# A three-block mixer kernel on one core: norm sums by row or by tile, bank and queue order at four norm starts, and the order of work in the mixers' loop

## The reference

```
def rms_norm(x, w):
    xf = x.astype(jnp.float32)
    y = xf * lax.rsqrt(jnp.mean(xf * xf, axis=-1, keepdims=True) + EPS)
    return (y * w.astype(jnp.float32)).astype(x.dtype)
```

```
    inner = jnp.einsum('bnqhd,bnkhd->bnhqk', q, k) * decay
    inner = jnp.einsum('bnhqk,bnkhe->bnqhe', inner, v)
    cross = jnp.einsum('bnqhd,hq,bnhde->bnqhe', q, xi, prev)
    o = (inner + cross).reshape(B, S, H, dh)
    mu = jnp.mean(o, axis=-1, keepdims=True)
    var = jnp.mean((o - mu) ** 2, axis=-1, keepdims=True)
    o = ((o - mu) * lax.rsqrt(var + EPS)).reshape(B, S, H * dh)
```

```
    y_diag = jnp.einsum('bcgls,bcghls,bcsghp->bclghp', cb, seg, xdt)
    states = jnp.einsum('bclgn,bcghl,bclghp->bcghpn', Bm, decay_states, xdt)
    y_off = jnp.einsum('bclgn,bcghpn,bcghl->bclghp', Cm, prev, jnp.exp(cs))
    y = y_diag + y_off + D_skip.astype(f32).reshape(G, HG)[:, :, None] * x
```

## Time and profile before

| | |
|---|---|
| three runs | 5030.29, 5031.72 (median), 5037.49 us |
| profiled execution's own time, and its span | 5030.29 us, 5028.6 us |
| TensorE busy, mean granted clock | 4354.2 us of the span, 0.920 |
| VectorE, ScalarE, GpSimd busy | 1853.5, 1297.2, 1080.6 us |
| norm starts: first product matmul at | 13.97, 1191.03, 2239.51, 2980.92 us |
| mixers' loop | from about 949 to 1082 us |

### The profile page before, as it was taken

The page is one execution under the profiler, slowest core; times in us unless marked ns, Lnnn a source line. Parts: engine busy times, 40 slices in busy tenths (PEclk is TensorE's granted clock), DMA queues, the critical chain, the costliest instruction groups (busy, mean ns, idle before and its releaser), DMA issues. The chain is left out here.

```text
span 5028.6 us, 55972 instructions
## 1 busy us (share of the span) xinstructions
PE 4354.2 (87%) x21658; PEld 3547.6 (71%) x21658; DVE 1853.5 (37%) x3177; ACT 1297.2 (26%) x2236; POOL 1080.6 (21%) x544
## 2 busy tenths in 40 slices
PE   8996979869875888389999999999899999889287
PEld 6885767657753887267878778888788888667165
DVE  3030656643465674314424413000233333314522
ACT  3120323432114444221000022121244444401111
POOL 2220000331312565022212212221111111113120
PEclk9997989979987999799999999999999999787588
DMA  3233011321323110211111112231334333423421
GB/s 118 99 142 89 20 34 27 95 79 42 135 92 122 45 28 16 80 51 51 42 51 51 34 51 97 94 145 71 91 105 110 88 100 91 151 71 109 135 82 78
DMA packets 268402, 403.66 MB, mean 80 GB/s; under 512 B 52597, under 2 KB 179446, under 8 KB 262650
## 3 DMA queue, kind: packets, MB, share of 16 engines
q1 hardware_dynamic: 222330, 308.97, 19.8%
q10 hardware_dynamic: 43632, 86.53, 4.6%
q0 software_dynamic: 2192, 4.80, 0.4%
HBM read 281.46 MB, written 118.75 MB: 80 GB/s over the span
## 5 line engine op out<-in xcount | busy, mean ns | idle before, releaser
L136 POOL TENSOR_TENSOR weights_wlow<-weights_raw,weights_whigh 128x1024 fp32r<-128x1024 f32 (+1 forms) x236 | 663.9, 2834 | 2603.2 <-ACT weights_whigh L127 2603.0
L244 PE MATMUL acc<-h_high_half,weights_whigh 128*128 128x512 f32 x1440 | 565.8, 393 | 81.4 <-POOL weights_wlow L136 69.7
L127 ACT ACTIVATE weights_whigh<-weights_raw 128x1024 fp32r<-128x1024 f32 (+1 forms) x236 | 267.7, 1164 | 1345.3 <-PE acc L244 734.2
L244 PE MATMUL acc<-h_high_half,weights_wlow 128*128 128x512 f32 x1440 | 564.3, 392 | 0.0
L244 PE MATMUL acc<-h_low_half,weights_whigh 128*128 128x512 f32 x1440 | 564.3, 392 | 0.0
L244 PEld LDWEIGHTS acc<-h_high_half,weights_whigh 128*128 128x128 f32 x1440 | 273.2, 190 | 142.8 <-POOL weights_wlow L136 71.3
L3127 PE MATMUL acc<-h_high_half,weights_whigh 128*128 128x512 f32 x768 | 332.4, 433 | 0.0
L247 PE MATMUL acc<-weights_whigh,h_high_half 128*128 128x512 f32 x768 | 302.2, 393 | 14.0 <-PEq L187 14.0
L244 PEld LDWEIGHTS acc<-h_high_half,weights_wlow 128*128 128x128 f32 x1440 | 273.0, 190 | 57.0
L244 PEld LDWEIGHTS acc<-h_low_half,weights_whigh 128*128 128x128 f32 x1440 | 272.7, 189 | 57.1
L3127 PE MATMUL acc<-h_low_half,weights_whigh 128*128 128x512 f32 x768 | 302.9, 394 | 0.0
(11 more groups left out here) (533 smaller groups left out, 8241.9 us busy)
## 6 DMA issues: line engine op xcount, KB each, us to landing
weights_raw<-w_cols SPq DMA_DIRECT2D x94, 512.0 KB, 5.0
weights_raw<-w_ff SPq DMA_DIRECT2D x64, 512.0 KB, 3.7
weights_raw<-w_rows SPq DMA_DIRECT2D x30, 1024.0 KB, 7.2
att<-gated_result_sb SPq DMA_DIRECT2D x96, 130.0 KB, 2.2
merge_o_sb<-att SPq DMA_DIRECT2D x24, 520.0 KB, 5.4
weights_raw<-w_out SPq DMA_DIRECT2D x24, 512.0 KB, 3.7
cols<-cols1p_out ACTq DMA_DIRECT2D x40, 256.0 KB, 2.1
rows<-rows1p_out ACTq DMA_DIRECT2D x32, 256.0 KB, 2.6
```

Source lines behind the costliest of these rows:

```text
L127: self.core.nc.scalar.activation(high[p][:, half * (KC // 2):(half + 1) * (KC // 2), :], raw[half], ACT.Copy).then_inc(self.core.sem("roun ...
L136: self.core.nc.gpsimd.tensor_tensor(low[p][:, hs, :], raw[half], high[p][:, hs, :].bitcast(F32), ALU.subtract).then_inc(self.core.sem("wei ...
L244: mm = nc.tensor.matmul(core.acc[b][:, :], wt[p][:, k, c * P:(c + 1) * P], h[:, k, half * HALF:(half + 1) * HALF], start=first, stop=final)
```

## The change

It has three parts, in two classes of place.

1. *The sums of a norm.* `late.sums` now takes a 128 by 128 tile of the squares as stationary operand and one or two columns of `per` as the moving one, 8 tiles for each of the 8 steps, into columns of bank 4, which `clear_sums` zeroes first. The sums come out as columns, so the copy of the rows and `late.turn` are gone. A step's order is high by high, high by low, low by high, and TensorE waits for `weights_wlow` ahead of the first step.
2. *Order and waits at a norm start.* SP issues both blocks of weights before the transfers of x (norm1). The third block waits for `emptied[b]` without the subtraction.
3. *The mixers' loop.* `turn_mixed(t - 1)` stands at the end of tile t, into banks 4 and 7, and waits for `xb`; `turn(t)` waits for `copied`, which DVE sets at the end of `rest(t - 2)`. `rest` stands ahead of `steps_in` on DVE, the squares and one more small step are DVE's, `within` stands ahead of `statistics`, the sum of squares ahead of `renew`. ACT no longer squares and has no `warm` root. The retention update goes to bank 2, `retained` is set before it.

```
@@ dense
             if late:
                 for it in range(there, 2):
                     load(it, 0, it)
-                    if it == 0:
-                        late.sync(sp)
+                late.sync(sp)
...
-                    pe.wait_ge(emptied[b], it + at[f"emptied_{b}"] - (1 if late and it == 2 else 0))
+                    pe.wait_ge(emptied[b], it + at[f"emptied_{b}"])
...
-                pe.wait_ge(core.sem("rounded"), at["rounded"] + 2)
+                pe.wait_ge(split, at["weights_split"] + 2)
...
-                late.wait(pe, "ready", 1)
+                late.clear_sums(pe)
                 for k in range(KC):
                     late.wait(pe, "highs", k + 1)
                     through_banks(0, k, 0, high, whigh)
+                    through_banks(0, k, 1, high, wlow)
                     late.wait(pe, "lows", k + 1)
-                    through_banks(0, k, 1, low, whigh)
-                    if k == 0:
-                        pe.wait_ge(split, at["weights_split"] + 2)
-                    through_banks(0, k, 2, high, wlow)
+                    through_banks(0, k, 2, low, whigh)
...
-                    if k == KC // 2:
-                        late.turn(pe)
@@ LateNorm
+    def clear_sums(self, pe):
+        self.wait(pe, "ready", 1)
+        self.core.nc.tensor.matmul(self.core.acc[4][:, 0:KC * self.n], self.core.ones[:, :], self.zeros[:, :], start=True, stop=True)
...
-        for h in range(2):
-            mm = self.core.nc.tensor.matmul(self.core.acc[4 + h][0:n, :], self.per[:, k, :], self.squares[k % 4][:, h * HALF:(h + 1) * HALF],
-                                            start=k == 0, stop=k == KC - 1)
+        for t in range(NT):
+            mm = self.core.nc.tensor.matmul(self.core.acc[4][:, n * t:n * t + n], self.squares[k % 4][:, t * P:(t + 1) * P],
+                                            self.per[:, k, :], start=False, stop=True, skip_group_check=True)
         mm.then_inc(self.sem("summed"), 1)
...
@@ mixers, TensorE
                 def turn(t):
-                    pe.wait_ge(sig(f"inputs{t % 2}"), 96 * (t // 2 + 1))
+                    if t >= 2:
+                        pe.wait_ge(sig("copied"), t - 1)
...
                     pe.wait_ge(sig("mixed"), f + 1)
                     pe.wait_ge(sig("sparse"), f + 1)
+                    pe.wait_ge(sig("xb"), min(f + 2, NT))
...
                     turn(t)
-                    if t >= 2:
-                        turn_mixed(t - 2)
                     retain(t)
                     carry(t)
-                turn_mixed(NT - 2)
+                    if t:
+                        turn_mixed(t - 1)
                 turn_mixed(NT - 1)
@@ mixers, ScalarE
-                    act(sq[:, 0:MIX], dif[:, :], ACT.Square)
-                    act(sq[:, MIX:2 * MIX], ro[f % 2][:, :], ACT.Square).then_inc(sig("squared"), 1)
...
-                    act(warm[:, :], core.eps[:, :], ACT.Sqrt).then_inc(sig("warm"), 1)
@@ mixers, VectorE
-                    stt(out=o, in0=bc(mu[:, :], HD), scalar=-1.0 / HD, in1=o, op0=ALU.mult, op1=ALU.add).then_inc(sig("centred"), 1)
+                    then(ts(mu[:, :], mu[:, :], 1.0 / HD, None, ALU.mult))
+                    tt(o, o, bc(mu[:, :], HD), ALU.subtract).then_inc(sig("centred"), 1)
...
+                    tt(sq[:, MIX:2 * MIX], ro[f % 2][:, :], ro[f % 2][:, :], ALU.mult)
+                    then(tt(sq[:, 0:MIX], dif[:, :], dif[:, :], ALU.mult))
...
```

More of the change, by code:

```diff
@@ L401 @@
 class LateNorm:
-    NAMES = ("ready", "highs", "lows", "squared", "summed", "rows", "sums", "rooted", "second", "turned", "spread", "copied", "passed", "scaled",
+    NAMES = ("ready", "highs", "lows", "squared", "summed", "rooted", "second", "turned", "spread", "copied", "passed", "scaled",
              "highs_again", "lows_again", "step")
@@ L424, in finish @@
         n = self.n
-        for name, count in (("ready", 1), ("highs", KC), ("lows", KC), ("squared", KC), ("summed", KC), ("rows", 2), ("sums", 1), ("rooted", n),
+        for name, count in (("ready", 1), ("highs", KC), ("lows", KC), ("squared", KC), ("summed", KC), ("rooted", n),
                             ("second", n - 1), ("turned", n), ("spread", n), ("copied", 2 * n), ("passed", KC * self.renew),
@@ L438, in sums @@
         self.wait(pe, "squared", k + 1)
-        for h in range(2):
-            mm = self.core.nc.tensor.matmul(self.core.acc[4 + h][0:n, :], self.per[:, k, :], self.squares[k % 4][:, h * HALF:(h + 1) * HALF],
-                                            start=k == 0, stop=k == KC - 1)
+        for t in range(NT):
+            mm = self.core.nc.tensor.matmul(self.core.acc[4][:, n * t:n * t + n], self.squares[k % 4][:, t * P:(t + 1) * P],
+                                            self.per[:, k, :], start=False, stop=True, skip_group_check=True)
         mm.then_inc(self.sem("summed"), 1)
-    def turn(self, pe):
-        n = self.n
-        self.wait(pe, "rows", 2)
-        for t in range(NT):
-            mm = self.core.nc.tensor.transpose(self.core.acc[6][:, n * t:n * t + n], self.squares[2][0:n, t * P:(t + 1) * P],
-                                               self.core.ident[0:n, 0:n])
-        mm.then_inc(self.sem("sums"), 1)
     def spread(self, pe):
@@ L487, in scalar_roots @@
     def scalar_roots(self, a):
-        act, sums = self.core.nc.scalar.activation, self.core.acc[6][:, 0:KC * self.n].rearrange("p (t n) -> p t n", n=self.n)
+        act, sums = self.core.nc.scalar.activation, self.core.acc[4][:, 0:KC * self.n].rearrange("p (t n) -> p t n", n=self.n)
         self.wait(a, "summed", KC)
-        for h in range(2):
-            act(self.squares[2][0:self.n, h * HALF:(h + 1) * HALF], self.core.acc[4 + h][0:self.n, :], ACT.Copy
-                ).then_inc(self.sem("rows"), 1)
-        self.wait(a, "sums", 1)
         act(self.r[:, :], sums[:, :, 0], ACT.Sqrt, bias=self.core.eps[:, 0:1], scale=1.0 / D).then_inc(self.sem("rooted"), 1)
@@ L539, in vector_first @@
         if self.n == 2:
-            sums = self.core.acc[6][:, 0:KC * 2].rearrange("p (t n) -> p t n", n=2)
+            sums = self.core.acc[4][:, 0:KC * 2].rearrange("p (t n) -> p t n", n=2)
             then(tt(self.v[:, :], self.r[:, :], self.r[:, :], ALU.mult))
@@ L1623, in square @@
                     act(rstd[:, :], stat[:, :], ACT.Sqrt, scale=1.0 / HD, bias=core.eps[:, 0:1]).then_inc(sig("root"), 1)
-                    a.wait_ge(sig("warm"), f + 1)
-                    act(warm[:, :], core.eps[:, :], ACT.Exp).then_inc(sig("warm_exp"), 1)
+                    act(warm[:, :], core.eps[:, :], ACT.Exp)
                 c.wait(a)
@@ L1700, in rest @@
                         part = slice(f * P, (f + 1) * P)
-                        ins = tt(low[:, 4 * h:4 * h + 4, part], core.acc[2 + 5 * h].rearrange("p (c t) -> p c t", c=4),
+                        ins = tt(low[:, 4 * h:4 * h + 4, part], core.acc[4 + 3 * h].rearrange("p (c t) -> p c t", c=4),
                                  high[:, 4 * h:4 * h + 4, part].bitcast(F32), ALU.subtract)
@@ L1789, in _ @@
                         scores(t)
-                        steps_in(t)
                     if t >= 2:
                         rest(t - 2)
+                    if t < NT:
+                        steps_in(t)
                     if t:
                         centre(t - 1)
+                    if t < NT:
+                        within(t)
+                    if t:
                         statistics(t - 1)
                     if t < NT:
-                        within(t)
                         renew(t)
                         outputs(t)
-                    if t:
-                        sums(t - 1)
-                    if t + 1 < NT:
-                        widen(t + 1)
+                        if t + 1 < NT:
+                            widen(t + 1)
                     if t:
```

33 lines of the change are left out of this document (11 added, 22 removed).

## The result

The changed kernel takes 5122.63 us, median of 4 runs (5117.61 to 5125.02), against 5031.39 us before (4 runs, 5030.29 to 5037.49): ratio 1.0177, 95% interval 1.0160 to 1.0195, 91 us slower. The forecast was 5143 us, 113 slower. Every term but the one taken as nothing had the right sign; the sum was some 20 us too high, and one reason behind it was wrong.

The account below looks back on a forecast made before the run. TensorE, busy 87% of the span, was taken as the bound, except in the mixers' loop, where VectorE is. Terms 0 + 46 - 3 + 23 + 9 + 38 = 113 us on 5030.3 gave 5143 us, range 5083 to 5178.

Parts of the forecast that it names:

- the one taken as nothing: Norm starts: the instructions of the sums by tile, taken as 0 us, bounds -31 to +1 us.
- Part 1, instructions, 0 us: Norm starts: 32 records at 0.112 us, 3.58 us a step against 3.52, so the new sums' instructions cost nothing.
- The other side: Rival, norm sums: a short matmul costs what it streams, 0.05 us a record; 5037 us, chance 0.03.
- Part 1, clock, +46 us: Norm starts: few-column sums lose the full clock, 2.9 us in each of 16 steps; bounds 0 and 99 us.
- -3: Norm starts: transposes leave TensorE's queue and low parts are not awaited in the first step; bounds -5 and 0 us.
- The clock holds, 5097 us: Rival, norm sums: full clock needs only a busy TensorE, so the sums by tile cost nothing; chance 0.27.
- Third block, +23 us: Four norms' third blocks: TensorE waits for the bank's emptying, 16.2 us, plus 6.8 of clock; bounds 14 and 30.
- The clock's 6.8 us: Third blocks: each wait exceeds the 2.63 us gap that halved the clock, so 1.7 us is added four times.
- norm1, +9 us: norm1's start: x issued behind both blocks' weights, TensorE starts near 23 us instead of 13.97; bounds 6 and 13.
- Loop, +38 us: Mixers' loop: transposes, scores, segments wait for DVE's last step; +3.4 to +7.2 us a tile, bounds 23 to 46.
- Short loop term: Rival, mixers' loop: bound elsewhere, DVE has slack, 38 us fall to 10; 5115 us, chance 0.09.
- half clock through all four steps: Rival, norm starts: long matmuls never bring the clock back between groups, 46 becomes 99; 5196 us, chance 0.06.

Follow-up runs that it names:

- e5: Kernel before with sums of squares by tile, each sums matmul streaming 64 columns instead of one or two, clearing matmul widened to 512: 5019.96 us, -13.2.
- e1: Kernel before with only the sums of squares by tile (one or two columns streamed) and the clearing matmul: 5059.61 us, +27.9.
- e9: Whole changed kernel, but each matmul of the sums streams 64 columns instead of one or two: 5087.91 us, +55.0 on the kernel before.
- e2: Kernel before with only the third block waiting for its own bank's emptying (subtraction gone): 5049.06 us, +17.3.
- e10: Kernel before with only DVE's products for TensorE (`within`) put ahead of `statistics` in the mixers' loop: 5024.95 us, -8.0.
- e11: Kernel before with the loop's transposes last and the squares and mean's division on DVE, none of the loop's other new orders: 5071.80 us, +38.9.
- e4: Kernel before with only the changed kernel's mixers' stage: 5065.08 us, +33.4.

## Why the prediction was right, and where it was off

- **Bound and sum.** Norms and loop are the places, each term is paid in full, and all of them add: shown by four kernels with one part each. 113 forecast, 91 measured, 87 from the parts.
- **Part 1, instructions, 0 us.** Right: 0.109 us a record in e5 at the full clock, against 0.112 taken. The other side's 0.05 is refuted.
- **Part 1, clock, +46 us, and -3.** The mechanism was right as to the fall, with TensorE busy all the time. The size was off: 43 with the 3, measured 27.9 alone by medians, 34.6 by place, and 29.6 by place in the changed kernel. Both terms have a share. The clock's was 41 us (e1 against e5), not 46. "16 steps of 2.9 us" failed at the first step of each norm, which already ran at half clock in the kernel before, behind its gap, and cost 0.2 to 0.6 us; the other steps cost 2.2 to 2.6. (At norm1 the trace has no clock for it, but its four matmuls take 2.04 us, the pace of the half clock.) Half of this stood in my own rows: the 1193 to 1196 stretch at 0.50 is that first step. And what leaves the queue was worth 6.5 us by place, 13.2 in the total, not 3 (e5). In the changed kernel one of norm3's groups kept the full clock besides; that was luck.
- **Its reason.** "Matmuls with few columns do not get the full clock there" was read from a stage that had entered at half clock. With 64 columns, groups entered at the full clock kept it, and the cost went (e5, e9). The forecast for one or two columns came out right, by luck, on a row that did not carry it. Had the change streamed 64 columns, the same argument would have been wrong by 40 us.
- **The clock holds, 5097 us.** Refuted by 2.00 of 2.00 us busy at 0.54. Where a group streams 64 columns, it is what happens.
  The Trainium skill ("TensorE: Matmul & The Clock Gate", section "Why this matters for your kernels") asks for a TensorE kept busy; the trace agrees for 64 columns entered at the full clock, and not for one or two, nor for the compression stage's 63 entered at half clock.
- **Third block, +23 us.** The wait was right to a tenth of a microsecond (a gap of 4.47, of which 0.41 were there before, against 3.97 forecast). The clock's 6.8 us were right by place too: 7.3 in e2, 9.9 in the changed kernel. The median of 17.3 in all is within the bounds and lower than the places add up to, 23.7. The premise behind them, that a gap of 2.6 us halves the clock, doesn't hold everywhere: behind 2.14 us it fell at e9's norm3 and not at its norm2.
- **norm1, +9 us.** Right: 8.5 alone; 22.22 us for the start in the changed kernel, 23 forecast.
- **Loop, +38 us.** Chain right, 33.4 measured, 30.8 by the loop's length in the changed kernel; this is the other term that was too high. Per tile +4.9 us, between the 3.4 and 7.2 of the forecast: transposes and scores at half clock took the 1.7 us each that I took, but the segments took 2.1 us (from 1048.47, L1413's start, to 1050.57) instead of 3.6, eight records of L1416 in 1.05 us being the pace of the full clock, and the way from there to `centre` 3.15 instead of 3.9. "Nothing is saved" was wrong for what follows it: `within` ahead of `statistics` saves some 5 to 8 us alone (e10), and the other orders together 9 (e11 against e4), which I had not priced.
- **Short loop term and half clock through all four steps.** Neither: e4 gives 33, and the clock is 1.00 again inside each group.

## What to carry to other kernels

A row at a low clock tells whether the work raised the clock only together with what came before it: look at the idle time ahead of the stretch before it is used as a price for work that enters at the full clock. If a gap already halves a step, a second cause of half clock costs little in that step (here 0.2 to 0.6 us instead of 2.2 to 2.6). When a total's interval is as wide as the term, compare the same two matmuls in both traces. In a loop whose pace one engine sets, move nothing behind that engine's last step which its next step needs; and its consumers' inputs go ahead of its bookkeeping.

## What the runs showed of the hardware

The same 32 full weight loads, 0.11 us apart at the full clock, kept 2.4 GHz with 64 columns streamed between them, and with one or two the clock fell to 1.2 GHz in or right behind each of e1's 16 groups, TensorE counted as busy in both; more work on TensorE was 40 us faster. Behind the same 2.14 us of idling the clock was 1.00 at one norm and 0.50 at another of one execution (e9). And 512-column sums with bfloat16 operands ran at 0.24 us a record, one record a matmul, where float32 took 0.44 and two.
